# Four merge-gate units of a decoder trunk computed as two more seven-product pairs before the attention, and the probabilities weighted by GpSimd

## The reference

```
h = rmsnorm(x, norm1_g)
proj = h @ w_in                      # q, keys and values, gates, pool input, 2 x 1024 merge columns
merge = sigmoid(proj[..., o_merge:]) # 2 x 1024 columns
for each of 8 blocks of 128 queries, each of 2 groups of 4 heads:
    p_c, p_s, p_w = softmax of compressed, selected and window scores
    o = g0 * (p_c @ v_c) + g1 * (p_s @ v_s) + g2 * (p_w @ v_w)
x = x + (merge[0] * (o @ w_attn_proj) + merge[1] * b) @ w_out
```

## Time and profile before

| | |
|---|---|
| median of 3 runs | 1386.23 us (1385.8 to 1388.58) |
| span of the profiled execution | 1385.2 us |
| PE busy | 1374.7 us (99%), granted clock 1.000 |
| DVE busy | 1039.6 us (75%) |
| ACT busy | 739.7 us (53%) |
| POOL busy | 207.9 us (15%) |

### The profile page before, as it was taken

One profiled execution on the slowest core, in us unless ns is written; L12 is line 12 of the kernel. 1 busy time (PEld: TensorE's weight loads), 2 busy tenths in 40 slices (PEclk: granted clock), 3 DMA queues, 4 the chain that ended last, 5 costly groups with the idle time before them and its releaser, 6 DMA issues.

```text
span 1385.2 us, 19117 instructions
## 1 busy us (share of the span) xinstructions
PE 1374.7 (99%) x6581; PEld 1138.1 (82%) x6581; DVE 1039.6 (75%) x2050; ACT 739.7 (53%) x1437; POOL 207.9 (15%) x203
## 2 busy tenths in 40 slices
PE   9999999999999999999999999999999999999998
PEld 7788778888888888788888888888888888888887
DVE  6977487888788878856568877778695968777764
ACT  6433446666666666522235655545454645555464
POOL 5233100101010100000230030212213040302100
PEclk9999999999999999999999999999999999999999
DMA  7446531222222121754232184654738192846553
GB/s 223 123 152 178 160 91 54 65 62 65 60 68 61 48 68 47 236 182 151 76 94 89 47 146 97 129 107 85 136 82 162 49 157 69 150 94 122 106 168 122
DMA packets 162141, 151.75 MB, mean 110 GB/s; under 512 B 12691, under 2 KB 125127, under 8 KB 162048
## 3 DMA queue, kind: packets, MB, share of 16 engines
q1 hardware_dynamic: 145920, 121.20, 28.9%
q0 software_dynamic: 16128, 29.37, 14.4%
HBM read 94.43 MB, written 56.10 MB: 109 GB/s over the span
## 4 chain that ended last, share of the span: by engine, by line
PE 96%; DVE 1%; ACT 1%; DMA 1%; issue 1%; POOL 0%; ACTq 0%; POOLq 0%; DVEq 0%
PE psU L2282 5%; PE psU L2283 5%; PE psU L2284 5%; PE psX L2552 5%; PE psU L2735 4%; PE psU L2737 4%; PE psU L2736 4%; PE psX L2282 4%; PE psX L2283 4%; PE psX L2284 4%; PE psU L2772 4%; PE psU L2774 4%; PE psU L2773 4%; PE psX L2735 3%; PE psX L2737 3%; PE psX L2736 3%
## 5 line engine op out<-in xcount | busy, mean ns | idle before, releaser
L1038 POOL DMA_DIRECT2D residual_scratch<-csum x112 | 98.3, 915 | 483.0 <-DVE csum L2166 415.7
L1989 DVE TENSOR_TENSOR ring_lo<-raw,ring_hi 128x512 fp32r<-128x512 f32 x150 | 103.0, 686 | 62.6 <-ACT ring_hi L1334 62.4
L1334 ACT ACTIVATE ring_hi<-raw 128x512 fp32r<-128x512 f32 x150 | 92.6, 624 | 64.0 <-PE psU L2774 23.3
L1221 ACT ACTIVATE pth<-psX 128x512 fp32r<-128x512 f32 x148 | 88.1, 595 | 71.8 <-PE psX L2552 71.1
L1887 DVE TENSOR_TENSOR ptl<-psX,pth 128x512 fp32r<-128x512 f32 x132 | 90.4, 688 | 25.5 <-ACT pth L1221 23.9
L1213 ACT ACTIVATE prob<-prob,nb 128x640 f32<-128x640 f32 (+7 forms) x128 | 93.4, 730 | 25.3 <-DVE nb L1861 25.2
L2282 PE MATMUL psX<-ahi,whi 128*128 128x512 f32 x256 | 103.3, 403 | 0.1
L2283 PE MATMUL psX<-alo,whi 128*128 128x512 f32 x256 | 100.9, 394 | 0.0
L2284 PE MATMUL psX<-ahi,wlo 128*128 128x512 f32 x256 | 100.5, 393 | 0.0
L2552 PE MATMUL psX<-ident,prob 128*128 128x128 f32 x592 | 89.5, 273 | 0.3 <-DVE ptl L1887 0.2
L1010 POOL TENSOR_TENSOR wlo<-wraw,whi 128x1024 fp32r<-128x1024 f32 x14 | 33.6, 2402 | 329.6 <-DVE prob L1875 329.6
(11 more groups left out here) (377 smaller groups left out, 4043.5 us busy)
## 6 DMA issues: line engine op xcount, KB each, us to landing
raw<-in_w_ff_dram SPq DMA_DIRECT2D x120, 256.0 KB, 4.3
residual_scratch<-csum POOLq DMA_DIRECT2D x112, 256.0 KB, 5.9
wraw<-in_w_in_dram SPq DMA_DIRECT2D x21, 512.0 KB, 4.1
gate_scratch<-zst SPq DMA_DIRECT2D x32, 256.0 KB, 3.8
mg<-gate_scratch SPq DMA_DIRECT2D x16, 512.0 KB, 3.4
proj_scratch<-stage SPq DMA_DIRECT2D x30, 256.0 KB, 2.0
duo_w<-in_w_in_dram SPq DMA_DIRECT2D x20, 256.0 KB, 4.6
xt<-in_x_dram SPq DMA_DIRECT2D x8, 512.0 KB, 7.9
```

Of the source, the lines that this page charges most:

```text
L1038: pool.dma_start(resid[rows, cols], sums[b][e][:], accum_op=ALU.add).then_inc(added[b][e], 16)
L1334: nc.scalar.activation(weights_of(g)[0], raw_of(g), ACT.Copy).then_inc(w_hi, 1)
L1989: nc.vector.tensor_tensor(lo, raw_of(g), hi.bitcast(f32), ALU.subtract).then_inc(w_lo, 1)
```

## The change

Merge units 12 to 15 leave the attention. They become two more pairs (`Z_DUOS`) after the five of the input stage; ACT takes their tanh (`early_tanh`) and SP stores them at once. The attention keeps 12 merge units (`LATE`), and how many of their gate steps an iteration gets is a table (`Z_SHARE`) in place of 16 for each. The lead ahead of an iteration's first turn is cut to what the stage has. POOL multiplies the probabilities by the inverse sum and the gate in one instruction (`weights` on POOL), where DVE did it in two steps; DVE keeps the inversion (`factors`) and, of each iteration's last head, the selected branch, for which PE waits by a semaphore of its own (`p_last`). Some semaphores of loads and stores are merged, with the same waits. The core of the diff:

```diff
-    DUOS = ((2, 3), (U_KC, U_VC), (U_KS, U_VS), (U_KW, U_VW), (U_Q + 1, U_Q + 2))
+    LATE = 12
+    HEAD_DUOS = ((2, 3), (U_KC, U_VC), (U_KS, U_VS), (U_KW, U_VW), (U_Q + 1, U_Q + 2))
+    Z_DUOS = tuple((UNITS + q, UNITS + q + 1) for q in range(LATE, 2 * KT, 2))
+    DUOS = HEAD_DUOS + Z_DUOS
...
-    N3 = NZ + 2 * KT
+    N3 = NZ + LATE
...
-        Z_STEPS = 2 * KT - 2
-
-        GATE_LEAD = [2 if it % 2 == 0 and it < Z_STEPS else 1 if it <= Z_STEPS else 0 for it in range(NIT)]
+        GATE_LEAD = [2 if it % 2 == 0 and it < NIT - 2 else 1 if it < NIT - 1 else 0 for it in range(NIT)]
+
+        Z_SHARE = (9, 14, 9, 13, 10, 13, 9, 14, 9, 14, 9, 13, 10, 13, 8, 6)
...
+        def gate_ends():
+
+            ends, past = [], 2 * KT
+            for c in range(GR * NIT):
+                wanted = 2 * KT + sum(Z_SHARE[:c // GR]) + (Z_SHARE[c // GR] * (c % GR + 1) + GR - 1) // GR
+                past = max(past, min(wanted, KT * (past // KT + 1), 2 * KT * LATE - 3))
+                ends.append(past)
+            return ends
+
+        Z_ENDS = gate_ends()
+        Z_TAIL = 2 * KT * LATE - Z_ENDS[-1]
...
-            if it == 0:
-                return 1, *((0, 5), (5, 8), (8, 12), (12, 2 * KT))[r]
-            if it < Z_STEPS:
-                return it + 1, KT // 2 * r, KT // 2 * (r + 1)
-            if it == Z_STEPS:
-                return Z_STEPS + 1, 2 * r, 2 * r + 2
-            return Z_STEPS + 1, 2 * GR + (r + 1 if r else 0), 2 * GR + r + 2
+            c = it * GR + r
+            return Z_ENDS[c - 1] if c else 2 * KT, Z_ENDS[c]
+
+        def gates_past(it, r):
+
+            done = [c for c in range(2 * KT, 2 * KT * LATE, KT)
+                    if gate_share(it, r)[0] < c + KT <= gate_share(it, r)[1]]
+            return [(c // (2 * KT), c // KT % 2) for c in done]
...
+                if u >= UNITS:
+                    done = 3 * (q - len(HEAD_DUOS))
+                    sp.wait_ge(z_early, done + 1)
+                    store_early(u, 0)
+                    sp.wait_ge(z_early, done + 2)
+                    store_early(v, 1)
+                    sp.wait_ge(z_early, done + 3)
+                    store_early(v, 0)
+                    sp.wait_ge(d_last, q + 1)
+                    store_early(u, 1)
+                    continue
...
-            for n in range(NZ + 2, N3):
+            def weights(it, r):
+
+                g, i = ITER[it]
+                head = g * GR + r
+                w, gate = rs[:, it % 2, r], gates[:, i, head]
+                row = PB[it % 2]
+                pool.wait_ge(w_ready, it * GR + r + 1)
+                for k, (lo, hi) in enumerate(branch_cols(i)[1:]):
+                    if k or r < GR - 1:
+                        pool.tensor_scalar(row[:, r, lo:hi], row[:, r, lo:hi], w[:, k + 1:k + 2], gate[:, k + 1:k + 2],
+                                           ALU.mult, ALU.mult)
+                lo, hi = branch_cols(i)[0]
+                pool.tensor_scalar(row[:, r, lo:hi].rearrange("p (c k) -> p c k", c=2),
+                                   cexp[:, r % 2:r % 2 + 1].broadcast_to([P, 2, CP]), w[:, 0:1], gate[:, 0:1],
+                                   ALU.mult, ALU.mult).then_inc(p_ready, 1)
+
+            def gate_lo(q):
+
+                n = NZ + q
                 pool.wait_ge(w_hi, n + 1)
-                pool.wait_ge(p_ready, GR * (n - NZ - 1) + 1)
                 pool.wait_ge(w_lo, n)
                 nc.gpsimd.tensor_tensor(wlo[:, n % 2], wraw[:, n % 2], whi[:, n % 2].bitcast(f32), ALU.subtract).then_inc(w_lo, 1)
+
+            pool.wait_ge(misc_ev, N_MISC)
+            for r in range(GR):
+                weights(0, r)
+            gate_lo(2)
+            for it in range(NIT):
+                for r in range(GR):
+                    for q, h in gates_turn(it, r):
+                        if h and q + 2 < LATE:
+                            gate_lo(q + 2)
+                    if it + 1 < NIT and r:
+                        weights(it + 1, r - 1)
+                if it + 1 < NIT:
+                    weights(it + 1, GR - 1)
...
+                if unit >= UNITS and i == I_T4:
+                    nc.scalar.activation(dst, duo_bank(q, which), ACT.Tanh, scale=0.5).then_inc(d_last, 1)
+                elif unit >= UNITS:
+                    nc.scalar.activation(dst, duo_bank(q, which), ACT.Copy).then_inc(copied, 1)
+                else:
+                    nc.scalar.activation(dst, duo_bank(q, which), ACT.Copy,
+                                         scale=qscale[:, unit:unit + 1]).then_inc(d_last if i == I_T4 else copied, 1)
+
+            def early_tanh(q, c):
+
+                u, v = DUOS[q]
+                unit, h = ((u, 0), (v, 1), (v, 0))[c]
+                dst = stage[:, unit % 2, h * HALF:(h + 1) * HALF]
+                act.wait_ge(summed, 3 * q + c + 1)
+                nc.scalar.activation(dst, dst, ACT.Tanh, scale=0.5).then_inc(z_early, 1)
...
-                    if q == 4 and i == I_B22:
-                        split_hi(4, 0, raw_need(4), used=8, products=N_PROD * len(DUOS) - 1)
+                    if DUOS[q] in Z_DUOS and i in (I_T1, I_B22, I_T4):
+                        early_tanh(q, (I_T1, I_B22, I_T4).index(i))
+                    if q == len(DUOS) - 1 and i == I_B22:
+                        split_hi(4, 0, raw_need(4), used=8, products=N_PROD * len(DUOS) - 0)
...
-                link(nc.vector.reciprocal(w, esum[:, it % 2, r]))
-                link(nc.vector.tensor_tensor(w, gates[:, i, head], w, ALU.mult))
-                for k, (lo, hi) in enumerate(branch_cols(i)[1:]):
-                    nc.vector.tensor_scalar(row[:, r, lo:hi], row[:, r, lo:hi], w[:, k + 1:k + 2], None, ALU.mult)
-                lo, hi = branch_cols(i)[0]
-                nc.vector.tensor_scalar(row[:, r, lo:hi].rearrange("p (c k) -> p c k", c=2),
-                                        cexp[:, r % 2:r % 2 + 1].broadcast_to([P, 2, CP]), w[:, 0:1], None,
-                                        ALU.mult).then_inc(p_ready, 1)
+                nc.vector.reciprocal(w, esum[:, it % 2, r]).then_inc(w_ready, 1)
+                if r == GR - 1:
+                    dve.wait_ge(w_ready, it * GR + r + 1)
+                    lo, hi = branch_cols(i)[1]
+                    nc.vector.tensor_scalar(row[:, r, lo:hi], row[:, r, lo:hi], w[:, 1:2], gates[:, i, head, 1:2], ALU.mult,
+                                            ALU.mult).then_inc(p_last, 1)
...
-                        lead = 0 if r else 1 if it == NIT - 1 else GATE_LEAD[it]
+                        lead = min(0 if r else 1 if it == NIT - 1 else GATE_LEAD[it], g1 - g0)
...
+                        pe.wait_ge(p_last, it + 1)
```

More of the change, by code:

```diff
@@ L391, in hybrid_trunk @@
         fin_last = sem("fin_last")
-        st_out = [sem(f"st_out{c}") for c in range(4)]
         def raw_need(n):
@@ L802, in _ @@
                     load_q(it + 2)
-                if it < Z_STEPS:
-                    load_unit(NZ + it + 4)
-                    store_z(it + 1, 0)
+                for r in range(1, GR):
+                    for q, h in gates_turn(it, r):
+                        if h == 0 and q + 1 < LATE:
+                            load_unit(NZ + q + 3)
+                        store_z(q, h)
             zscr_m = zscr.rearrange("(m z p) t -> m p z t", z=2, p=P)
@@ L910, in _ @@
                     store_out(t + 1, c)
-            for c in range(4):
-                sp.wait_ge(st_out[c], 64)
+            for t in range(TT):
+                sp.wait_ge(row_io[t], ROW_STORED)
         @block.gpsimd
```

119 lines of the change are left out of this document (73 added, 46 removed).

## The result

| | before | changed |
|---|---|---|
| median | 1386.01 us (4 runs) | 1417.81 us (1416.1 to 1421.57, 4 runs) |
| span of the profiled execution | 1385.2 us | 1414.4 us |
| mean granted clock of PE | 1.000 | 0.997 |

The ratio is 1.0231, 95% interval 1.0214 to 1.0248: slower by 31.8 us. The prediction had the direction, but 1391 us and at most 1399. The profiled execution is 29.2 us longer than the one before (1414.4 against 1385.2); what follows accounts for these.

The account below looks back on a forecast made before the run. PE, busy 99%, was taken as the bound: -44.8 + 38.1 + 1.5 + 5.1 + 1.3 + 3.6 = +4.8 us on 1385.2 gives 1390.0, median 1391 us. Its own range was 1388 to 1396, the wider one 1381 to 1399.

Parts of the forecast that it names:

- The pairs: Two added pairs of 84 matmuls on PE, at 0.227 us each, add 38.1 us.
- The bridge: Between last pair product and first pool product, unit 4's split and one more tanh delay the values: 1.5 us.
- the upper bound of 2.5: Delay before the pool products if DVE's split of unit 4, moved behind the last product, comes last: 2.5 us.
- the reckoned path: ACT's split of unit 4, evacuation and one more tanh before the values' high part, starting about 168.3: 1.5 us later.
- POOL's price: POOL's weighting, priced at its one-input rate: 0.72 us for 640 columns, 0.29 for 120.
- the third rival: POOL multiplies at its two-input rate, so first turns come later: +19 us, 1405 us; chance 0.1.
- First turns and the start: PE waits at first turns of iterations 2, 8, 10, 14 (5.1 us) and at the attention's start (1.3 us).
- Turns with nothing between: Turns without gate steps between wait for two-bank reuse, in iterations 0, 2, 6, 10, 14: 3.6 us, bounds 2.8 to 6.
- the removed steps gain their full 44.8 us: 64 gate steps leaving the attention, at 0.70 us each, take 44.8 us from PE.
- The first, that cover suffices: Rival: relieved DVE delivers sooner, only PE's work and the bridge count, so faster: 1381 us; chance 0.2.
- the second, that waits and gain cancel: Rival: no collision between DVE and POOL, turns at the lower bound: +1.6 us, 1388 us; chance 0.25.
- the collision: DVE's selected branch of head 3 and POOL's weighting hold each other up: up to 0.65 us, half taken.

Follow-up runs that it names:

- e1: Changed kernel but all 16 merge units stay in the attention, four gate steps a stage; only the weighting moves to POOL: 1392.7 us (1.0049).
- e15: Changed kernel with four gate steps in every stage up to iteration 13, some computed more than once, its own steps by a more even table: 1438.5 us (1.0379).
- e7: Changed kernel with three of eight gate steps of each half of merge units 1 to 11 left out (66 steps, gates wrong): 1399.0 us (1.0095).
- e2: Changed kernel with its added pairs and table of gate steps, but DVE weights the probabilities as before: 1423.0 us (1.0261).
- e18: Changed kernel with a third table of gate steps by stage, and DVE in place of POOL splitting the merge gates' weights: 1403.2 us (1.0123).
- e9: Changed kernel with gate steps tabled by stage, and DVE's scaling of the maxima written with two tensor inputs in place of one: 1406.1 us.

## Why the prediction was wrong

**The pairs: right.** 38.1 us forecast; up to the last pair product 37.7 us were added.

**The bridge: right in size and in ACT's order, not in the wait.** 1.5 us forecast, 1.45 measured (39.15 - 37.7). The values' high part began at 205.89, where 168.3 + 37.7 = 206.0 had been reckoned. In the changed kernel, ACT, DVE and PE:

```profile
202.98 1.06 ACT L1140 ACTIVATE whi<-wraw 128x1024 fp32r<-128x1024 f32 x1 [4.09 <-PE psU L2592]
...
204.42 0.62 ACT L1265 ACTIVATE stage<-stage 128x512 f32<-128x512 f32 x1
...
205.89 1.07 ACT L1203 ACTIVATE vS<-psX 128x512 fp32r<-128x512 f32 x2
...
206.58 1.29 DVE L1728 TENSOR_TENSOR vS<-psX,vS 128x512 fp32r<-128x512 f32 x2
...
206.66 0.66 PE L2544 MATMUL psX<-ident,ldA 128*128 128x128 f32 x4 [1.75 <-DVE vC L1772]
207.41 1.10 PE L2537 MATMUL psX<-up,wp 128*128 128x512 f32 x2
```

PE waited 1.75 us for DVE's `vC`, and not for `vS`: DVE's split of unit 4 (204.07 to 205.30) stood ahead of it, the case for which the upper bound of 2.5 was there. The pool product then followed without a further wait, 0.83 us behind the start of `vS` on DVE (207.41 - 206.58), as it had before the change (168.26 - 167.42 = 0.84). So the reckoned path and the other one ended together, and that the sum fits to 0.05 us is partly luck.

**POOL's price: the class was right, the figure low.** Groups of the weighting, with mean ns before the bar's end:

```profile
L1074 POOL TENSOR_SCALAR prob<-prob,rs,gates 128x640 f32<-128x640 f32 x38 | 35.4, 936 | 28.3 <-DVE rs L1979 28.3
L1077 POOL TENSOR_SCALAR prob<-kC,rs,gates 128x128 f32<-128x128 f32 x64 | 30.2, 471 | 0.0
```

0.94 and 0.47 us, where 0.72 and 0.29 were taken; the two-input rate of the third rival would have been 1.5 us.

**First turns and the start: right in sum, by luck.** 5.1 + 1.3 = 6.4 us forecast, 5.9 measured, at the start of the attention and of iterations 2, 6, 8, 10 and 14:

```profile
247.43 0.66 PE L2659 MATMUL psX<-ident,prob 128*128 128x128 f32 x4 [1.47 <-POOL prob L1077]
...
291.88 1.52 PE L2659 MATMUL psX<-ident,prob 128*128 128x128 f32 x8 [2.25 <-POOL prob L1077]
...
389.82 0.66 PE L2659 MATMUL psX<-ident,prob 128*128 128x128 f32 x4 [0.53 <-POOL prob L1077]
...
431.75 0.66 PE L2659 MATMUL psX<-ident,prob 128*128 128x128 f32 x4 [0.66 <-POOL prob L1077]
...
474.67 0.47 PE L2389 MATMUL psX<-ahi,whi 128*128 128x512 f32 x1 [1.63 <-ACT zst L1341]
...
476.86 0.66 PE L2659 MATMUL psX<-ident,prob 128*128 128x128 f32 x4 [0.58 <-POOL prob L1077]
...
567.99 1.09 PE L2659 MATMUL psX<-ident,prob 128*128 128x128 f32 x8 [0.37 <-POOL prob L1077]
```

The sizes by place were not: iteration 2 paid 2.25 us for 1.3, iteration 10 0.58 for 2.0, iteration 14 0.37 for 0.95, and iteration 6, for which nothing was reckoned, 0.53. PE had been held up ahead of iteration 10 (1.63 us for a tanh at 474.67), so that it came later to the turn. (In the term for the start, 206.1 + 0.3 + 1.0 is 207.4 and not 207.5; it changes nothing.)

**"Turns with nothing between": this step failed.** It held 3.6 us for everything else in the attention, bounded by 6. The attention gave back 10.3 of 44.8 us, so 34.5 us of it are new; without the 5.9 at first turns, 28.6 stand where 3.6 stood. Nor did the waits it had named come where it had them: at the openings of iterations 2 and 6 no turn waited for a low part, at that of 14 one for 0.16 us; small ones came in iterations 0 and 6 (0.15, 0.16, 0.46), as it had them, but of the 5.2 us of such waits 4.1 stood in iterations 4 and 12 (2.08, 0.95, 1.10), which the sum had left out. The runs showed in its place: the gate steps were cover throughout the attention, not at its first turns alone. In each stage the chain scores, maxima, exponentials, high and low parts, tanh must run while PE has work, and where a stage has too few steps PE is through first. I had looked for slack at first turns only, and taken a stage elsewhere to be safe because before the change it showed no wait. No wait says that slack is not negative, not how much there is. Of the 28.6 us, waits with a name make 16.8 (9.1 + 5.2 + 1.9 + 0.6); all idle time of the window is 23.45, so 17.6 beside first turns. The rest, some 11 us, is not idle time in the records. Part of it is the clock: by the four windows of the last section PE lost up to 3.2 us to it (length times what the clock lacks to 1.00). For what remains, about 8 us, I have an account but no run: a record of a matmul lasts 0.16 us longer than the distance to the next (0.39 against 0.227), so a delay below that shows as busy.

**That the removed steps gain their full 44.8 us** was therefore wrong as well, as a way to reckon. A step taken out was worth 0.16 us (10.3 / 64) where it cost 0.70. This figure also carries POOL's weighting, which costs 6.6 us under full cover (e1, 2.4 of them at first turns). From e15 to the changed kernel a step was worth 0.28 us (20.7 / 73), and by e7 the next 66 are worth 0.28 each too.

**The rivals.** The first, that cover suffices, and the second, that waits and gain cancel, are refuted by 31.8 us. DVE's relief is real (997 us busy against 1040) and does not make up for the cover. The third, POOL at its two-input rate, did not occur. POOL's weighting is not the main cost either: e2, without it, is 5 us slower than the changed kernel. No kernel tried beats the one before; the best with the two added pairs and right results, e18, is 17 us slower.

## What to carry to other kernels

If the bounding engine is busy 99%, its work is worth its full price only as long as the others' latency chains have slack in each stage of the pipeline. So measure that slack before taking work away: take a little out of one stage and look at what comes back, or put filler into the stages of the new kernel and look at which waits close. When work must go, decide by stage where the rest stands; here the same 173 steps took 1405 or 1418 us.

## What the runs showed of the hardware

**PE's clock can fall after a wait of some 2 us.** Windows of the changed kernel behind the wait of 2.25 us at 291.88, and around that of 2.08 us at 347.47, ahead of which stood another of 0.92 at 344.89 (the clock is the third figure from the end):

```profile
291.88:295.72 3.84, 3.84 (x15) 2.98 (x16) 2.08 (x7) 2.16 (x5) 0.00 (x0) 0.57 0.73 190
295.72:297.00 1.28, 1.28 (x12) 1.27 (x10) 1.02 (x2) 1.28 (x6) 0.00 (x0) 0.97 0.49 147
```

```profile
347.40:350.00 2.60, 2.53 (x8) 2.24 (x9) 1.37 (x4) 0.92 (x3) 1.95 (x3) 0.50 0.00 0
350.00:352.00 2.00, 2.00 (x13) 1.67 (x11) 0.86 (x3) 0.00 (x0) 0.00 (x0) 0.90 0.00 0
```

0.50 is the level of 1.2 GHz. From 347.4 to 350.0 everything on PE ran at half speed (gate products 0.42 us apart where they are 0.23 elsewhere), so the wait cost more than its length. But it does not happen after each such wait. The bridge's wait of 1.75 us is the same in the changed kernel and in e15; here are both behind it, the changed kernel first:

```profile
208.50:210.50 2.00, 2.00 (x7) 0.80 (x5) 2.00 (x3) 2.00 (x7) 0.00 (x0) 1.00 0.91 238
```

```profile
208.20:210.20 2.00, 2.00 (x4) 0.69 (x3) 2.00 (x4) 2.00 (x7) 0.00 (x0) 0.50 0.87 223
```

In the changed kernel a wait of 1.80 us at 415.44 left it at 1.00 too. The Trainium skill, TensorE: Matmul & The Clock Gate, HAM oscillation, describes this trap, a clock that falls in an idle stretch, so that the work behind it starts slow; the trace agrees in two places, with 2.08 us of idle and a clock of 0.50 in the second. No run here separates its price from the rest.

**POOL and DVE can hold each other up, up to the end of an instruction.** A DVE instruction of 0.17 us took up to 2.40 us beside POOL's two-input split, in the form with one tensor input and in that with two (e9). In the other direction, POOL's L1061 took 2.12 us at 204.08 in the bridge, beside DVE's two-input split, where the same operation took 1.19 us before the change. The Trainium skill, SBUF — State Buffer, Who interferes with whom, says that a VectorE instruction contends both in its two-port modes and with two SBUF inputs against a GpSimd instruction that reads SBUF, and otherwise not. The runs agree: the scaling, the queries' low part and the weighting stalled, the reciprocals and all that read PSUM did not. I had priced the collision at one place and not followed which other DVE instructions would now stand beside the split.
